# A decoder step on one core: the first feed-forward products read the scaled residual before the second layer norm, and the norm is applied to their outputs

## The reference, cut to what matters

```python
ALPHA = (2 * DEPTH) ** 0.25      # DEPTH = 1, D_MODEL = 2048, D_FF = 5632

def layer_norm(x, g, b):
    mu = xf.mean(-1, keepdims=True)
    var = jnp.square(xf - mu).mean(-1, keepdims=True)
    return (xf - mu) * lax.rsqrt(var + LN_EPS) * g + b

def post_norm(x, sub, g, b):
    return layer_norm(ALPHA * x + sub, g, b)

def swiglu(h, w1, w2):
    gu = h @ w1
    return (jax.nn.silu(gu[..., :D_FF]) * gu[..., D_FF:]) @ w2

x = post_norm(x, cross_attend(x, ...), ln_g[l, 1], ln_b[l, 1])
x = post_norm(x, swiglu(x, ffn_w1[l], ffn_w2[l]), ln_g[l, 2], ln_b[l, 2])
```

## Time and profile before

| | us |
|---|---|
| median of 3 runs | 1637.1 |
| lowest, highest | 1633.76, 1639.01 |
| the profiled execution | 1636.82 |
| its span | 1634.9 |
| its mean granted TensorE clock | 0.984 |

### The profile page before, as it was taken

How to read it: one execution, slowest core, us unless ns; L and a number is a source line. 1 busy time by engine, 2 the same in 40 slices (tenths; PEclk the granted TensorE clock), 3 DMA queues, 4 the chain that set the end, 5 groups by cost and what they waited for, 6 DMA issues and landing times.

```text
span 1634.9 us, 35903 instructions
## 1 busy us (share of the span) xinstructions
PE 1555.5 (95%) x14713; PEld 1507.2 (92%) x14713; DVE 889.7 (54%) x1001; ACT 630.5 (39%) x693; POOL 189.4 (12%) x290
## 2 busy tenths in 40 slices
PE   7999999999889879999979999999999999999996
PEld 6998999999888779997869999999999999999996
DVE  3444646557743345674386666544454544454566
ACT  3434342343423443454363333333333333333344
POOL 0000202021697401001001000000000000000000
PEclk9999999999999999999989999999999999999998
DMA  8488878785799958555626776555555555555453
GB/s 330 159 330 327 310 271 341 288 320 193 223 264 263 308 221 309 179 173 202 220 81 236 244 263 237 196 183 179 181 180 180 180 181 180 180 180 180 165 183 117
DMA packets 104416, 365.14 MB, mean 223 GB/s; under 512 B 14369, under 2 KB 48490, under 8 KB 77290
## 3 DMA queue, kind: packets, MB, share of 16 engines
q1 hardware_dynamic: 89682, 322.66, 56.5%
q0 software_dynamic: 12528, 37.24, 6.7%
q10 hardware_dynamic: 2096, 3.70, 0.7%
HBM read 353.27 MB, written 10.47 MB: 222 GB/s over the span
## 4 chain that ended last, share of the span: by engine, by line
PE 75%; issue 8%; DVE 5%; ACT 4%; DMA 3%; SPq 2%; POOL 2%; POOLq 1%; ACTq 0%; DVEq 0%
PE psum_g L514 22%; PE psum_g L515 21%; PE psum_g L516 21%; PE M L1930 3%; PE M L1945 3%; DVE wl L499 2%; ACT wh L494 2%; DMA raw<-w_in_t 1%; ACT xf L1110 1%; PE psum_g L2235 1%; POOL pj L586 1%; SPq L612 1%; SPq L654 1%; DMA raw<-w_out_t 1%; POOLq L586 1%
## 5 line engine op out<-in xcount | busy, mean ns | idle before, releaser
L514 PE MATMUL psum_g<-xh,wh 128*128 128x264 f32 x2640 | 776.9, 294 | 38.6 <-DVE wl L499 14.9
L515 PE MATMUL psum_g<-xl,wh 128*128 128x264 f32 x2640 | 755.6, 286 | 0.0
L516 PE MATMUL psum_g<-xh,wl 128*128 128x264 f32 x2640 | 754.6, 286 | 0.0
L499 DVE TENSOR_TENSOR wl<-raw,wh 128x2048 fp32r<-128x2048 f32 (+1 forms) x223 | 503.7, 2259 | 382.1 <-ACT wh L494 381.9
L514 PEld LDWEIGHTS psum_g<-xh,wh 128*128 128x128 f32 x2640 | 504.4, 191 | 54.8 <-issue 32.4
L494 ACT CAST wh<-raw 128x2048 fp32r<-128x2048 f32 (+1 forms) x223 | 418.2, 1875 | 331.4 <-PE psum_g L516 280.1
L515 PEld LDWEIGHTS psum_g<-xl,wh 128*128 128x128 f32 x2640 | 505.0, 191 | 3.4 <-issue 3.1
L516 PEld LDWEIGHTS psum_g<-xh,wl 128*128 128x128 f32 x2640 | 502.4, 190 | 0.0
L514 PE MATMUL psum_g<-gh,wh 128*128 128x264 f32 x704 | 200.3, 284 | 0.0
L516 PE MATMUL psum_g<-gh,wl 128*128 128x264 f32 x704 | 199.4, 283 | 0.0
L515 PE MATMUL psum_g<-gl,wh 128*128 128x264 f32 x704 | 199.4, 283 | 0.0
(11 more groups left out here) (388 smaller groups left out, 1303.6 us busy)
## 6 DMA issues: line engine op xcount, KB each, us to landing
raw<-w_t SPq DMA_DIRECT2D x88, 1024.0 KB, 4.8
raw<-w_in_t SPq DMA_DIRECT2D x55, 1024.0 KB, 7.6
kring<-cache_k_t SPq DMA_DIRECT2D x96, 512.0 KB, 4.8
sraw<-cache_k_t SPq DMA_DIRECT2D x32, 512.0 KB, 6.0
raw<-w_out_t SPq DMA_DIRECT2D x16, 1024.0 KB, 4.9
raw<-w2a_t SPq DMA_DIRECT2D x16, 1024.0 KB, 4.8
raw<-w2b_t SPq DMA_DIRECT2D x16, 1024.0 KB, 4.8
raw<-w2c_t SPq DMA_DIRECT2D x16, 768.0 KB, 4.3
```

The lines of the kernel that those rows point to most:

```text
L499: eng.tensor_tensor(wl[:, u % 2, 0:nk], raw[:, u % 2, 0:nk], wh[:, u % 2, 0:nk].bitcast(F32), ALU.subtract).then_inc(raw_used, 1)
L514: nc.tensor.matmul(out, hi_w, x_hi(k), start=(k == order[0]), stop=False)
L515: nc.tensor.matmul(out, hi_w, x_lo(k), start=False, stop=False)
L516: last = nc.tensor.matmul(out, lo_w, x_hi(k), start=False, stop=(k == order[-1]))
```

## The change

The layer norm is linear in x once mean and deviation are known, so with r the residual before the norm,

    h @ W = rstd * ((g*r) @ W - mean * (g @ W)) + b @ W

- `raw_upper` and `raw_lower` make upper and lower parts of g*r, chunk by chunk, as xo's results arrive; chunks 0 to 3 go into a new tile `rx` (xo still reads the first chunks of `xh`), the others into `xh` and `xl`, which become two columns wider: the columns 264 and 265 hold g and b, so that each w1 product (266 columns) also gives g @ W and b @ W.
- `layer_norm(1)` goes. w1a's first eight units ("raw units") are written out, in eight banks, before the statistics are known; PE sums the chunks up after unit 2 and the squares after unit 3. The upper part of the weights is cast by ACT ahead of everything else in xo.
- After each w1 unit, ACT copies the two columns to `wgb` (`weight_sums`), and DVE's `evict` makes `tw` = (bank - mean * (g @ W)) * rstd, in two operations. ACT's `gate` applies SiLU to `tw` with b @ W as bias; DVE's `gated_pair` does what `gate_unit` did.
- x itself, which w2a adds onto, is normed in w2a: DVE subtracts the mean and multiplies by rstd (two operations a unit), ACT applies g and b.
- The state update moves from w1a to w1b.

```diff
-xh = sb("xh", [P, KC, T], F32R)
-xl = sb("xl", [P, KC, T], F32R)
+xh_wide = sb("xh", [P, KC, T + 2], F32R)
+xl_wide = sb("xl", [P, KC, T + 2], F32R)
+xh, xl = xh_wide[:, :, 0:T], xl_wide[:, :, 0:T]
...
+rx = sb("rx", [P, 2, 4, T + 2], F32R, sF)
+wgb = sb("wgb", [P, 8, 2], stack=sF)
+tw = sb("tw", [P, 2, T], stack=sF)
+fsum = sb("fsum", [P, 4, T], stack=sF)
...
+RH = lambda k: rx[:, 0, k] if k < 4 else xh_wide[:, k]
+RL = lambda k: rx[:, 1, k] if k < 4 else xl_wide[:, k]
+RAW_UNITS = 8
+BANKS = [M[:, 2], M[:, 3], M[:, 4], M[:, 5], psum_g[:, 0], psum_g[:, 1], M[:, 2], M[:, 3]]
+def ffn_bank(u, peeled):
+    return BANKS[u] if peeled else psum_g[:, u % 2]
...
+    def raw_upper(chunks):
+        for k in chunks:
+            ins = nc.scalar.activation(RH(k)[:, 0:T], xf[:, k], ACT.Copy, scale=ln_gb[:, 0, 1, k:k + 1])
+        ins.then_inc(r_act.sem, 1)
+    def raw_square(u):
+        nc.scalar.activation(xt[:, 4 * u:4 * u + 4], xf[:, 4 * u:4 * u + 4], ACT.Square).then_inc(r_act.sem, 1)
...
+    gb_columns = ln_gb[:, :, 1].rearrange("p c k -> p k c")
+    nc.scalar.copy(rx[:, 0, :, T:T + 2], gb_columns[:, 0:4])
+    nc.scalar.copy(xh_wide[:, 4:KC, T:T + 2], gb_columns[:, 4:KC]).then_inc(r_act.sem, 1)
     for u in range(4):
         upper_next(act, turn, u)
...
-    layer_norm(1)
-    act.preload_act_table(ACT.Silu)
+        if u:
+            act.wait_ge(psum_free, 4 * turn + u + 2)
+            raw_upper(range(4 * u - 4, 4 * u))
+            raw_square(u - 1)
+    wait(act, r_dve, "half")
+    raw_upper((12, 13))
+    turn, n = STAGES["w1a"]
+    upper_next(act, turn, 0)
+    act.wait_ge(psum_free, 4 * turn + 2)
+    raw_upper((14, 15))
+    raw_square(3)
+    def weight_sums(turn, u, pair, peeled):
+        unit_done(act, turn, u)
+        if not peeled:
+            act.wait_ge(gu_done, pair - 1)
+        nc.scalar.copy(wgb[:, u], ffn_bank(u, peeled)[:, T:T + 2]).then_inc(wg_done, 1)
+    def gate(slot, unit_, pair, first):
+        act.wait_ge(fx_done, unit_ + 1)
+        if not first:
+            act.wait_ge(gu_done, pair)
+        nc.scalar.activation(sg[:], tw[:, 0], ACT.Silu, bias=wgb[:, slot, 1:2]).then_inc(sg_done, 1)
+    for u in range(RAW_UNITS):
+        if u:
+            upper_next(act, turn + u // 4, u % 4)
+        if u == 4:
+            wait(act, r_dve, "vmax")
+            nc.scalar.activation(rstd[:], rstd[:], ACT.Ln, bias=LN_EPS).then_inc(r_act.sem, 1)
+            wait(act, r_act, "log")
+            nc.scalar.activation(rstd[:], rstd[:], ACT.Exp, scale=-0.5).then_inc(r_act.sem, 1)
+            act.preload_act_table(ACT.Silu)
+        elif u == 5:
+            gate(0, 0, 0, True)
+        elif u == 6:
+            gate(2, 2, 1, False)
+        elif u == 7:
+            gate(4, 4, 2, False)
+        weight_sums(turn, u, u // 2, True)
+    gate(6, 6, 3, False)
     for s1_, s2_, first, nk in GROUPS:
         turn, n = STAGES[s1_]
-        with act.Fori(0, n) as i:
+        with act.Fori(RAW_UNITS // 4 if s1_ == "w1a" else 0, n) as i:
             for u in range(4):
                 upper_next(act, i + turn, u)
-                if u % 2 == 0:
-                    unit_done(act, i + turn, u)
-                    act.wait_ge(psum_free, i * 4 + (4 * turn + u + 2))
-                    nc.scalar.activation(sg[:], psum_g[:, 0, 0:T], ACT.Silu).then_inc(psum_free, 1)
+                if u % 2:
+                    gate(u - 1, i * 4 + (2 * first + u - 1), i * 2 + (first + u // 2), False)
+                weight_sums(i + turn, u, i * 2 + (first + u // 2), False)
+        turn, n = STAGES[s2_]
+        last = s2_ == "w2c"
+        if not last:
+            with act.Fori(0, n) as i:
+                for u in range(4):
+                    upper_next(act, i + turn, u)
+                    if s2_ == "w2a":
+                        m = xf[:, ds(i * 4 + u, 1)].rearrange("p a n -> p (a n)")
+                        act.wait_ge(scl_done, i * 4 + (u + 1))
+                        nc.scalar.activation(m, m, ACT.Identity, bias=ln_gb[:, 1, 1, ds(i * 4 + u, 1)],
+                                             scale=ln_gb[:, 0, 1, ds(i * 4 + u, 1)]).then_inc(aff_done, 1)
...
+    def raw_lower(chunks, name):
+        wait(dve, r_act, name)
+        for k in chunks:
+            ins = nc.vector.scalar_tensor_tensor(RL(k)[:, 0:T], xf[:, k], ln_gb[:, 0, 1, k:k + 1],
+                                                 RH(k)[:, 0:T].bitcast(F32), ALU.mult, ALU.subtract)
+        ins.then_inc(r_dve.sem, 1)
...
     turn, n = STAGES["xo"]
     for u in range(3):
         lower_next(dve, turn, u)
+        if u:
+            raw_lower(range(4 * u - 4, 4 * u), f"h{u - 1}")
         unit_done(dve, turn, u)
         for at_, banks in (((4 * u, M[:, 0:4, 0:T]),) if u % 2 == 0 else
                            ((4 * u, M[:, 4:6, 0:T]), (4 * u + 2, psum_g[:, :, 0:T]))):
...
+    lower_next(dve, turn, 3)
+    raw_lower(range(8, 12), "h2")
     wait(dve, x_pe, "half")
...
+    raw_lower((12, 13), "h3")
     unit_done(dve, turn, 3)
     nc.vector.scalar_tensor_tensor(xf[:, 14:16], xf[:, 14:16], ALPHA, psum_g[:, :, 0:T], ALU.mult,
                                    ALU.add).then_inc(psum_free, 1)
...
-    layer_norm(1)
+    raw_lower((14, 15), "h4")
+    turn, n = STAGES["w1a"]
+    lower_next(dve, turn, 0)
...
+    def evict(turn, u, unit_, pair, peeled):
+        h = u % 2
+        dve.wait_ge(wg_done, unit_ + 1)
+        if not (peeled and u < 2):
+            dve.wait_ge(gu_done if h else sg_done, pair)
+        nc.vector.scalar_tensor_tensor(tw[:, h], mean[:], wgb[:, u, 0:1], ffn_bank(u, peeled)[:, 0:T], ALU.mult,
+                                       ALU.add).then_inc(psum_free, 1)
+        dve.wait_ge(psum_free, turn * 4 + (u + 3))
+        nc.vector.tensor_tensor(tw[:, h], tw[:, h], rstd[:], ALU.mult).then_inc(fx_done, 1)
+    def gated_pair(u, unit_, pair, j):
+        half = (u // 2) % 2
+        dve.wait_ge(fx_done, unit_ + 1)
+        dve.wait_ge(sg_done, pair + 1)
+        dve.wait_ge(gl_done, pair + 1)
+        nc.vector.scalar_tensor_tensor(gu[:, half], tw[:, 1], wgb[:, u, 1:2], sg[:], ALU.add, ALU.mult).then_inc(gu_done, 1)
+        dve.wait_ge(gu_done, pair + 1)
         nc.vector.tensor_scalar(gh[:, ds(j, 1)].rearrange("p a n -> p (a n)"), gu[:, half], 1.0, None,
                                 ALU.mult).then_inc(gh_done, 1)
+        dve.wait_ge(gh_done, pair + 1)
         nc.vector.tensor_tensor(gl[:, ds(j, 1)].rearrange("p a n -> p (a n)"), gu[:, half],
                                 gh[:, ds(j, 1)].bitcast(F32).rearrange("p a n -> p (a n)"),
                                 ALU.subtract).then_inc(gl_done, 1)
+    wait(dve, r_dve, "half")
+    dve.wait_ge(psum_free, 4 * turn + 2)
+    first_sum(xf, fsum[:])
+    lower_next(dve, turn, 1)
+    other_sums(("s1", "s2", "s3"), xf, fsum[:])
+    lower_next(dve, turn, 2)
+    wait(dve, r_act, "q3")
+    first_sum(xt, xt[:, 0:4])
+    other_sums(("p1", "p2", "p3"), xt, xt[:, 0:4])
+    lower_next(dve, turn, 3)
+    wait(dve, x_pe, "sum")
+    nc.vector.tensor_scalar(mean[:], M[:, 0, 0:T], -1.0 / D_MODEL, None, ALU.mult).then_inc(r_dve.sem, 1)
...
+    lower_next(dve, turn + 1, 0)
+    wait(dve, r_act, "rstd")
+    for u in range(RAW_UNITS):
+        evict(turn, u, u, u // 2, True)
+        if u % 2:
+            gated_pair(u, u, u // 2, u // 2)
+        if u == 1:
+            lower_next(dve, turn + 1, 1)
+        elif u == 5:
+            lower_next(dve, turn + 1, 2)
+        elif u == 6:
+            lower_next(dve, turn + 1, 3)
...
     for s1_, s2_, first, nk in GROUPS:
+        turn, n = STAGES[s1_]
+        states = s1_ == "w1b"
+        with dve.Fori(2 // 2 if s1_ == "w1a" else 0, n // 2) as i:
+            for s in range(2):
                 for u in range(4):
+                    lower_next(dve, i * 2 + (turn + s), u)
+                    unit_, pair = i * 8 + (2 * first + 4 * s + u), i * 4 + (first + 2 * s + u // 2)
+                    evict(i * 2 + (turn + s), u, unit_, pair, False)
                     if u % 2:
+                        gated_pair(u, unit_, pair, i * 4 + (2 * s + u // 2))
+                    if states and u == 0:
+                        dve.wait_ge(h_in[s], i * 16 + 16)
+                        nc.vector.tensor_tensor(state[:, s], state[:, s], per_head(1, i * 2 + s), ALU.mult).then_inc(h_dve.sem, 1)
...
+                    if s2_ == "w2a":
+                        nc.vector.tensor_tensor(m, m, mean[:], ALU.add).then_inc(ctr_done, 1)
+                        dve.wait_ge(ctr_done, i * 4 + (u + 1))
+                        nc.vector.tensor_tensor(m, m, rstd[:], ALU.mult).then_inc(scl_done, 1)
+                    onto_residual(i, u, m, KC)
...
+    def raw_ready(k):
+        if k == 0:
+            wait(pe, r_dve, "gb")
+            wait(pe, r_dve, "l2")
+        elif k in (12, 14):
+            wait(pe, r_dve, f"l{k // 2 - 3}")
+    for u in range(RAW_UNITS):
+        pe.wait_ge(raw_used, turn * 4 + (u + 3))
+        if u == 2:
```

(15 more changed lines are left out.)

145 lines of the change are left out of this document (60 added, 85 removed).

## The result

| | us |
|---|---|
| before, median of 6 runs | 1637.08 |
| after, median of 6 runs | 1644.77 (1642.99 to 1647.65) |
| ratio after to before, 95% interval | 1.0054 [1.0041, 1.0067] |
| the profiled execution of after, its span, its clock | 1645.82, 1643.9, 0.988 |

What follows compares the result with a forecast made beforehand. PE was taken to bound the kernel (95% busy), the second layer norm's idle times being the exception. Terms -10.2 + 3.5 + 5.2 + 0.5 = -1.0 us took 1637.1 to 1636.1; range 1629 to 1647, the forecast's own 1631.5 to 1641.

Steps and rivals of the forecast that it cites:

- gain at unit 7: w1a's first eight units: early start makes unit 7 end at 887.6 despite a 6.2 us PE idle: 10.2 us gained.
- mark 897.8: Time at which w1a's unit 7 would end in the kernel before, the mark to beat.
- two more columns, 80 units: w1 units after the first eight: 0.45 ns a column, 0.9 ns a product, 3.5 us lost (2.1 by the other slope).
- new eviction in w1b: w1b: state operation between gated pair and subtraction makes it 0.65 late once a turn, eight turns, 5.2 us (bounds 0 to 8).
- first unit of w2a, and the rest: w2a's first unit: new operations stand behind the last gated pair, subtraction 3.8 to 6.1, 0.5 us once.
- I take nothing: Products reading x at a stride of 266 elements: no cost counted; 1 ns each in 164 units would be 7.9 us.
- rival 4: Products reading xh slow down on the wider stride, 1 ns each: 1644 us; sign: first stages' products slower than 0.1208; chance 0.05.
- x was to be 6.16: w1b: x is when DVE's subtraction ends after a unit's end on PE; 6.16 against a bound of 5.51, 0.65 late.
- Rival 1: w1b: DVE's chain fits, or columns cost their lower bound; 4.7 to 7.6 us faster, 1629.5 to 1632.4; chance 0.22.
- rival 2: All w1 stages: DVE becomes the bound once x is over 5.5; with x = 5.7, 1647 us; chance 0.13.
- Rival 3: w1a's start: chunks or sums come late, half or all of the 10.2 us gone, 1641 to 1646; chance 0.07.

Runs made afterwards that it cites:

- order_fix: Changed kernel with, in w1a's first eight units, DVE's subtraction for unit 7 earlier and ACT's gate of unit 4 ahead of unit 8's cast: 1636.81 us, ratio 0.9998.
- own266: Changed kernel with w1's operand packed on its own at stride 266, all earlier stages at stride 264 again: 1643.61 us, ratio to before 1.0054.
- both: Changed kernel with the edits of order_fix and states_w2b together: 1632.65 us, ratio to before 0.9981.
- states_w2b: Changed kernel with DVE's state operations moved out of w1b's units into w2b's: 1640.26 us, ratio to before 1.0020.
- widths: Kernel before at stride 264, first layer's products 260 columns wide in w1a's loop, 266 in w1b, 272 in w1c: 1646.61 us, ratio 1.0060.
- widths_more: Kernel before at stride 264, first layer's products 268 columns wide in w1a's loop, 262 in w1b, 288 in w1c: 1654.15 us (1 run).
- one_wide: Kernel of both with w1's operand packed at stride 272 and the two columns only in the first of each chunk's three products: 1625.23 us, ratio to before 0.9935.
- stride_only: Kernel before with chunks of xh and xl 266 elements apart instead of 264, products still reading 264 columns: 1647.63 us, ratio 1.0071.

## Why the prediction was wrong

By the steps of its sum, with the profiled execution of after against that of before (9.0 us):

| step | forecast | measured | from |
|---|---|---|---|
| gain at unit 7 | -10.2 | -8.0 | unit 7's end at 889.8 (0.08 ahead of the copy at 889.88), forecast 887.6, mark 897.8 |
| two more columns, 80 units | +3.5 | +10.1 | 80 x 48 x 2.64 ns |
| new eviction in w1b | +5.2 | +5.2 | 8 turns x 0.65 |
| first unit of w2a, and the rest | +0.5 | +1.7 | what is left of 9.0 |

- **Two more columns: the step that failed.** The prediction took 0.45 ns a column, from the slope between 264 and 512 columns, with 0.27 (256 to 264) as the lower and nothing above it as the upper bound. Every slope had 264 as one end. The runs show that 264 at stride 264 is a low point: 262 columns take longer, 268 lie on a line that passes 1.8 ns above it. Every step off that point that the change could have taken with three wide products costs 2.6 to 3.3 ns (266 columns at strides of 266, 264 and 272). This term alone takes the forecast from 1636 to 1643.
- **The stride, "I take nothing".** The text gave it 1 ns as a rival (rival 4) and a chance of 0.05. By itself it costs 1.9 ns in w1 and 1.7 in the early stages. In w1 it costs nothing on top of the width (2.6 for both, 3.2 for the width). So rival 4 was right that a wider stride slows products, and its sign (products of the first stages slower than 0.1208) is there. Its total of 1644 is luck: it has 1 ns in all 164 units, while w1's 88 have 2.6 by width and stride together, and of the early stages' price only 0.5 us is seen in the kernel's time.
- **Gain at unit 7: the mechanism was right to tenths.** Forecast idle 6.2, found 6.05 in the row and 6.3 between the starts; forecast 24 slow products and 2.4 us, found the clock at 0.50 for 27 products; the order of ACT's and DVE's rows was as worked out. order_fix took it away and measured its price, 8.0 us. The 2.2 us that are missing of the gain came in at the front (unit 0 ended 1.5 late, at 835.7 for 834.2, as xo's first result was 1.6 late) and by the wider products of these eight units (8 x 48 x 1.7 ns = 0.65). One row was read wrongly, without harm: the low clock at 848.49 was put down to the 4.40 us of idle time ahead of it, but the products from 840.71 on, behind 5.42 us of idle time, were at 0.220 us already.
- **The eviction in w1b was right.** x was to be 6.16 and 0.65 too late, once in four units. Found: the turn is 0.65 longer than in w1a, eight waits, the chain nearly as forecast (gh 0.65 behind gu for 0.58, gl 0.42 behind gh, the state operation 0.36 behind gl), and none in w1a's and w1c's loops, as forecast for x = 5.07 against 5.51. Rival 1 falls, and rival 2 (a bound in all w1 stages) too. That the 0.65 came out to the hundredth is in part luck: the subtraction ends at 1167.76, x = 6.27 behind a unit that ended at 1161.49 (0.08 ahead of ACT's copy at 1161.57), 0.11 more than forecast, while wider units moved the bound from 5.51 to 5.61 (two units of 5.925, less 0.06, less the 6.18 from the start at 1167.81 to that unit's end).
- **What a dependent operation costs** is less settled than the prediction had it. In w1b's loop gh starts 0.15 us after gu has ended and gl 0.12 after gh; in the written-out units (877.47 to 878.33) the same two start 0.04 and 0.03 after. An operation that needs nothing of the one before starts 0.07 ahead of its end (1164.34). So about half of the price belongs to the loop and not to the dependence. The listings of the two places differ in one thing, register and wait instructions of their own ahead of gh and gl in the loop; that they are the cause was not tested.
- **Rival 3** (no early start) fell: w1a's first product came within 1.9 us of the forecast (829.55 for 827.65).
- **The rest.** The late subtraction at w2a's entry is there, with a wait of 0.18. There is a second one at w2c's entry (0.76), where units have 12 chunks and are shorter; the prediction had w2a only. What is left of the 1.7 was not followed up.
- **Before xo** the changed kernel was 3.3 us late in this profile (the last cast ahead of xo's first result starts at 806.92, before at 803.59). Of that, 0.5 to 0.7 us arose in the last 117 us and is the stride's for the most part (see own266). The rest can't be told from the spread of executions: at the same cast the profiles of order_fix, both and states_w2b, whose code is that of the changed kernel there, lie at +3.6, +3.4 and +0.5, and those of widths and widths_more, with the code of before, at -0.1 and -2.6.

## What to carry to other kernels

A product's time is no straight line in its columns near a width that happens to be cheap: before an operand is widened by two columns in thousands of products, measure exactly that width at exactly that stride, and have an upper bound in the sum that no neighbouring row excludes. If extra columns are needed, put them into as few of the products as possible: with one wide product of three the mean fell from 124.1 to 122.0 ns. And when an order is written by hand, look at what the preparation of the next weights stands behind: here it stood behind a pair that waited for a gate, and the gate behind a cast that waited for PE. Breaking that chain gave 8 us, of which 6 were idle time and the rest the lower clock behind it.

## What the runs showed of the hardware

Products in float32r of 128 x 128 weights with the given number of columns, at full clock, in ns from start to start:

| columns | stride 264 | stride 266 | stride 272 |
|---|---|---|---|
| 260 | 120.0 | | |
| 262 | 121.4 | | |
| 264 | 120.8 | 122.8, 122.9 | 121.0 to 122.0 (estimate from one_wide) |
| 266 | 124.0 | 123.5, 123.8 | 124.1 |
| 268 | 124.3 | | |
| 272 | 126.1 | | |
| 288 | 132.8 | | |

- From 268 to 288 columns the slope is 0.42 ns, which is one column in each cycle at 2.4 GHz. The Trainium skill (TensorE: Matmul & The Clock Gate, "Wait — 56ns, not 53.3ns?") has this slope and a fixed part of 2.5 ns; in these traces the fixed part is 12.8 ns at 288 (132.8 - 120.0), 13.2 at 266 and 10.8 at 264, all at the stride of 264. It is not constant: the 512 columns of rows 9, at 232.5, have 19.2.
- Why 264 columns are cheap at the stride of 264 and not at 266 stays open: blocks of 8 columns and blocks of 64 bytes were tried as explanations, and neither fits the table. The traces show that these means are averages over places. In before, each of a unit's 48 products has its own distance to the next, from 116 to 129 ns, the same to 0.2 ns in every unit of w1a's loop; the three products of a chunk take 357 to 370 ns, and the series repeats after eight chunks (363, 366, 357, 358, 368, 361, 370, 357). At the stride of 266 (stride_only) the distances are as fixed, but nothing repeats within the sixteen chunks, and they take 357 to 378. So the place of a run does matter, in a way that blocks of 64 bytes don't describe; no run moves the place and keeps width and stride.
- After an idle time of 6.05 us PE came back at a granted clock of 0.50, for 27 products; after waits of 0.2 to 1.1 us in the same stage it did not fall.
